# A mixed feed-forward whose ScalarE and VectorE read a step's banks first and split its weights second

## The chip, the cores and the metric

One core of a Trainium2 chip runs the whole program. The metric is the time of one execution in microseconds (us) of device time; the table below gives the median of several executions, and one further execution was profiled. TensorE (PE) does the matmuls, VectorE (DVE) and ScalarE (ACT) the elementwise work, GpSimd (POOL) some sums, and SyncE (SP) issues the loads from memory (HBM) into on-chip buffers.

## The reference, cut to what matters

Two model blocks run on 512 tokens of 1024 channels, in 32-bit floats. The part that the change touches is the feed-forward of the first block, with 4096 hidden channels:

```python
h = rmsnorm(x, norm_mlp_w[l]) * (1.0 + sc2) + sh2
ff = jnp.square(jax.nn.relu(h @ mlp_w1[l])) @ mlp_w2[l]
x = x + g2 * ff
```

Mixers stand before it and the whole second block behind it. Those stages stay as they are.

## The kernel before

**Precision by splitting.** Each 32-bit operand is split in two: ScalarE writes the rounded high part (`w_hi`, line 568 in the feed-forward), VectorE subtracts it from the original to get the low part (`w_lo`, line 577). PE then does three matmuls for each product (lines 484 to 486: high times high, low times high, high times low). So no weight can be used before ScalarE and then VectorE have passed over it.

**Items.** PE works through a list, ITEMS. Six "whole" items compute hidden tiles 0 to 5 (128 channels each; 24 matmuls of 512 columns). The other 26 hidden tiles are made in 13 pairs, 3 to 15, by a scheme that takes seven smaller products ("part" items 1 to 7, of 12 matmuls of 256 columns) for what would else be eight. Between the parts stand "down" items, which multiply finished hidden tiles with the second weight matrix (12 matmuls of 512 columns). A pair runs in this order: part 1, part 2, down, part 5, down, part 6, down, part 7, down, part 3, part 4. After pair 15 twelve down items remain.

**Buffers.** `raw` holds four tiles of 512 KB as they come from memory. SP issues their loads strictly in order, and each waits until the old contents of its place are split (and, for the first matrix, summed by GpSimd into `wsums`, which parts 3, 5, 6 and 7 use). Among the first loads in this stage SP's queue also holds eight loads of another matrix (`ada_a`, `ada_b`), each of which waits for a `gate_tile` on VectorE (line 2652, `acc<-ada,c_act,acc`). `w_hi` and `w_lo` have eight slots; a whole item takes two, the others one. `made_at` gives, at each item, the splits to be done in that step: those of the item seven slots ahead. The split waits only for the item that last used the slot, which is the one just before the item of the step. So it can run while PE is still on the item of the step.

**Bank reads.** PE sums into PSUM banks (`banks`). At a whole item ScalarE waits for PE to end it, then applies relu (L1915), squares (L1876) and makes the high part `hid_hi` (L1882). VectorE makes `hid_lo` of the tile before and then does a `gate_tile`. At parts 1, 5 and 6 ScalarE copies a bank to `snaps` (L1894); at parts 2, 7 and 3 VectorE adds a bank and a snap into `zt` (L2665, "block"). At part 3 and part 4 ScalarE does relu, square and `hid_hi` of a hidden tile. At a down item VectorE adds the bank onto `xT` (L2668). PE waits in turn: part 6 for the block of part 2, part 4 for the block of part 7, and part 1 of pair 3 for the relu of whole item 5 (its banks are 3 to 5). Between the first down item and part 5 of pair 3, PE sums the result of all eight `gate_tile`s (L790).

**Order.** Every engine's instructions are in program order, and a wait blocks all that stands behind it on its engine. In each step both ScalarE and VectorE first do the splits of the step and then its bank reads.

Of the kernel before, what the change touches and what calls it, by code (L numbers as in the profile page):

```python
# [211 lines left out]
def build(nc, a, out):  # L212
    with ExitStack() as ctx:
# [225 lines left out]
        def raw_wait(eng, d):  # L439
            eng.wait_ge(raw_in[d % RING], 16 * (d // RING + 1))  # L440

        def hi_unit(act, u, i=0):

            d = raw_index(u)
            act.wait_ge(raw_in[d % RING], 16 * (d // RING + 1) + 16 * i)
            if u >= RING:
                act.wait_ge(w_used, u - RING + 1 + RING * i)
            if U_V <= u < U_V + RING:
                act.wait_ge(f_used, SLOTS_END - SLOTS + 2 * (u - U_V + 1))
            src, dst = raw[:, d % RING, :], w_hi[:, u % RING, :]  # L450
            if u == 2:
                for s, t in index_parts(src, dst):
                    ins = act.activation(t, s, ACT.Copy)
                ins.then_inc(split_hi, 1)
            else:
                act.activation(dst, src, ACT.Copy).then_inc(split_hi, 1)  # L456
# [66 lines left out]
        def is_sum(item):  # L523
            return item[0] == "part" and FORM[item[2]][0] == "S"

        def sum_at(name):
            return wsums[:, S_ORDER.index(name), :]

        def sum_count(p, name):
            return N_TSUM + 4 * (p - FIRST_PAIR) + S_ORDER.index(name) + 1  # L530
# [21 lines left out]
        def slot_hi(act, item):  # L552

            if item[0] == "value":
                hi_unit(act, U_V + item[1])
                return
            n = SLOT[item]
            if n < SLOTS:
                act.wait_ge(w_used, U_FF - RING + n // 2 + 1)
            else:  # L560
                act.wait_ge(f_used, n - SLOTS + (2 if item[0] == "whole" else 1))
            if is_sum(item):
                act.wait_ge(ff_summed, sum_count(item[1], FORM[item[2]]))
                src = sum_at(FORM[item[2]])
            else:
                raw_wait(act, ff_raw(raw_of(item)))
                src = raw_part(item)
            act.activation(in_slot(w_hi, item), src, ACT.Copy).then_inc(f_hi, size_of(item))  # L568

        def slot_lo(dve, item):  # L570

            if item[0] == "value":
                lo_unit(dve, U_V + item[1])
                return
            dve.wait_ge(f_hi, SLOT[item] + size_of(item))
            src = sum_at(FORM[item[2]]) if is_sum(item) else raw_part(item)
            dve.tensor_tensor(in_slot(w_lo, item), src, in_slot(w_hi, item).bitcast(F32), ALU.subtract).then_inc(f_lo, size_of(item))  # L577
# [934 lines left out]
        def _(act):  # L1512
# [383 lines left out]
            def last_rows(j):  # L1896

                act.wait_ge(x_new, X_FF + j + 1)
                if j >= 2:
                    act.wait_ge(sq_added, Q_FF + j - 1)  # L1900
                act.activation(sqb[:, j % 2, :], xT[:, j, :], ACT.Square).then_inc(sq_made, 1)
                act.wait_ge(sq2_added, max(j + 1, 2))
                act.activation(relu[:, j % 2, :], xT[:, j, :], ACT.Square,
                               scale=par[:, PCOL["final_norm_w"] + j:PCOL["final_norm_w"] + j + 1]).then_inc(sq1_made, 1)
                act.activation(h_hi[:, j, :], xT[:, j, :], ACT.Copy, scale=scale4[:, j:j + 1]).then_inc(h_hi_made, 1)

            for item, now in made_at():
                for what in now:
                    slot_hi(act, what)
                kind, g = item[0], item[1]  # L1910
                if kind == "whole":
                    used(act, item)
                    if g >= 4:
                        act.wait_ge(h_ready, H_HID + g - 3)
                    act.activation(zt[:, g % 4, :], banks[:, g, :], ACT.Relu).then_inc(evac, 1)  # L1915
                    squared(g)
                elif kind == "part":
                    i = item[2]
                    if (g, i) == (FIRST_PAIR, 1):
                        form_highs()  # L1920
                    if i in (1, 5, 6):
                        snap(g, i, {1: 0, 5: 1, 6: 2}[i])
                    if i == 3:
                        z = zt[:, 2 * g % 4, :]
                        act.wait_ge(ff_added, added(g, 3))
                        act.activation(z, z, ACT.Relu).then_inc(evac, 1)
                        squared(2 * g)
                    if i == 4:
                        z = zt[:, 2 * g % 4 + 1, :]
                        used(act, item)  # L1930
                        act.wait_ge(h_ready, H_HID + 2 * g - 2)
                        act.activation(z[:, HALF:], z[:, HALF:], ACT.Relu)
                        act.activation(z[:, 0:HALF], part_bank(g, 4), ACT.Relu).then_inc(evac, 1)
                        squared(2 * g + 1)
                elif g == 7:
                    last_rows(item[2])

            def v_roots():

# [197 lines left out]
        def _(dve):  # L2137
# [533 lines left out]
            def last_rows(j):  # L2671

                used(dve, ("down", 7, j))
                if j == 0:
                    dve.wait_ge(ff_x, N_DOWN)
                onto_x(j, LAST_BANK[j]).then_inc(x_new, 1)
                dve.wait_ge(sq_made, Q_FF + j + 1)
                dve.wait_ge(sq_added, Q_FF + j)
                dve.tensor_tensor(ssq[:, :], ssq[:, :], sqb[:, j % 2, :], ALU.add).then_inc(sq_added, 1)
                dve.wait_ge(sq1_made, j + 1)  # L2680
                dve.wait_ge(sq2_added, 2 + j)
                dve.tensor_tensor(relu2[:, 0, :], relu2[:, 0, :], relu[:, j % 2, :], ALU.add).then_inc(sq2_added, 1)
                dve.wait_ge(h_hi_made, H_SGU + j + 1)
                dve.scalar_tensor_tensor(h_lo[:, j, :], xT[:, j, :], scale4[:, j:j + 1], h_hi[:, j, :].bitcast(F32),
                                         ALU.mult, ALU.subtract).then_inc(h_ready, 1)

            for item, now in made_at():
                for what in now:
                    slot_lo(dve, what)
                kind, g = item[0], item[1]  # L2690
                if kind == "whole":
                    if g:
                        hidden_low(g - 1)
                    gate_tile(g)
                elif kind == "part":
                    i = item[2]
                    if i == 1:
                        if g == FIRST_PAIR:
                            hidden_low(WHOLE - 1)
                            gate_tile(6)  # L2700
                            gate_tile(7)
                            form_lows((0, 1))
                        else:
                            hidden_low(2 * g - 2)
                    if i == 2:
                        block(g, 2, zt[:, 2 * g % 4, 0:HALF], 0, 1)
                        if g == FIRST_PAIR:
                            form_lows((2, 3))
                        else:
                            hidden_low(2 * g - 1)  # L2710
                    if i == 7:
                        block(g, 7, zt[:, 2 * g % 4 + 1, HALF:], 1, 2)
                    if i == 3:
                        block(g, 3, zt[:, 2 * g % 4, HALF:], 2, 3)
                elif g < 6:
                    m = KT * g + item[2]
                    if m == 0:
                        mod_part(6, 5, 1)
                        dve.wait_ge(mod_ready, 7)
                    used(dve, item)  # L2720
                    if m >= KT:
                        dve.wait_ge(ff_x, m - KT + 1)
                    onto_x(item[2], 6 + m % 2).then_inc(ff_x, 1)
                elif item == ("down", 6, 4):
                    hidden_low(HIDDEN - 2)
                    hidden_low(HIDDEN - 1)
                    dve.wait_ge(h_ready, H_HID + HIDDEN)
                    dve.memset(relu2[:, 0, :], 0.0).then_inc(sq2_added, 2)
                elif g == 7:
                    last_rows(item[2])  # L2730

# [447 lines left out]
```

## Time and profile before

| | us |
|---|---|
| median of 3 executions | 1298.34 (1297.82 to 1301.42) |
| the profiled execution, device time | 1300.62 |
| its span in the trace | 1299.0 |
| the mixed feed-forward in it | about 327 to 702 |

The profiled execution lies 2.28 us above the median, and 1.62 us of it lie outside its span. All times of day below are microseconds from the start of the span of this one execution.

How to read it: a row of a timeline has the start, the duration, the engine, the line, the operation and its names (output, then inputs). In brackets stand how long the engine was idle just before it and what ended that wait. In a table of stretches, each engine has its busy time, and PEclk is the clock granted to TensorE as a share of its full speed (1.00 is 2.4 GHz, 0.50 is 1.2 GHz).

### The profile page before, as it was taken

The page shows a single profiled execution, that of the slowest core. Times are in us where ns is not written, and L with a number is a line of the kernel's source. Part 1 is how long each engine was busy: PE and PEld are TensorE (multiplying, and loading weights), DVE is VectorE, ACT ScalarE, POOL GpSimd, SP SyncE. Part 2 cuts the span into 40 slices and gives each one's busy share as a digit, 9 for nine tenths or more (in the row PEclk, how much of TensorE's full clock was granted, in tenths as well). Part 3 has the DMA queues.
Part 4 walks back from the last instruction along what each step waited for, and adds up shares of the span by engine and source line. Part 5 has one row for each costly group of instructions (what it writes and reads, how often), then busy time and mean ns, then how long its engine had stood idle before and what let it go on. Part 6 is the DMA issues. An engine that isn't in the chain of part 4 may idle for free.

```text
span 1299.0 us, 19391 instructions
## 1 busy us (share of the span) xinstructions
PE 1240.9 (96%) x7048; PEld 1034.9 (80%) x7048; DVE 906.1 (70%) x1418; ACT 645.2 (50%) x1026; POOL 195.4 (15%) x220
## 2 busy tenths in 40 slices
PE   4999999999969999999899999999999999999998
PEld 3777778888758889888888888888888887777786
DVE  6889997856766655555657697766366667987832
ACT  3585345523544545454455565333233346978723
POOL 7022210000723131322300000110011001000000
PEclk9999999999979999999999999999999999999999
DMA  9678843325533232323233232334323232333311
GB/s 365 188 192 168 177 103 106 118 85 160 160 112 113 70 113 82 114 82 113 82 114 103 74 101 81 88 90 121 91 82 96 81 111 80 94 93 109 98 65 65
DMA packets 181614, 147.40 MB, mean 113 GB/s; under 512 B 6490, under 2 KB 162321, under 8 KB 181536
## 3 DMA queue, kind: packets, MB, share of 16 engines
q1 hardware_dynamic: 174064, 134.40, 33.7%
q0 software_dynamic: 6272, 10.91, 4.5%
q8 instruction: 49, 0.80, 0.2%
q10 hardware_dynamic: 1200, 1.05, 0.2%
q14 instruction: 29, 0.24, 0.1%
HBM read 135.59 MB, written 2.10 MB: 106 GB/s over the span
## 4 chain that ended last, share of the span: by engine, by line
PE 54%; DVE 23%; ACT 9%; issue 7%; DMA 6%; POOL 1%; ACTq 0%; DVEq 0%; SPq 0%; POOLq 0%
PE banks L484 16%; PE banks L486 16%; PE banks L485 16%; DMA raw<-in_mlp_w 4%; DVE w_lo L577 4%; DVE w_lo L468 2%; ACT w_hi L456 2%; ACT w_hi L568 1%; DVE xT L2668 1%; DVE score L2301 1%; DVE m L2298 1%; DVE xc L2902 1%; ACT zt L1876 1%; DVE score L2284 1%; DVE zt L2665 1%
## 5 line engine op out<-in xcount | busy, mean ns | idle before, releaser
L484 PE MATMUL banks<-h_hi,w_hi 128*128 128x512 f32 (+1 forms) x740 | 283.9, 384 | 10.0 <-ACT zt L1915 8.7
L486 PE MATMUL banks<-h_hi,w_lo 128*128 128x512 f32 (+1 forms) x740 | 274.5, 371 | 0.0
L485 PE MATMUL banks<-h_lo,w_hi 128*128 128x512 f32 (+1 forms) x740 | 274.2, 371 | 0.0
L468 DVE TENSOR_TENSOR w_lo<-raw,w_hi 128x1024 fp32r<-128x1024 f32 x136 | 165.5, 1222 | 88.9 <-ACT w_hi L456 86.5
L456 ACT ACTIVATE w_hi<-raw 128x1024 fp32r<-128x1024 f32 x136 | 142.2, 1051 | 100.0 <-PE banks L486 78.2
L484 PEld LDWEIGHTS banks<-h_hi,w_hi 128*128 128x128 f32 x740 | 142.0, 192 | 42.8 <-issue 17.1
L577 DVE TENSOR_TENSOR w_lo<-raw,w_hi 128x512 fp32r<-128x512 f32 (+1 forms) x109 | 93.3, 866 | 113.5 <-ACT w_hi L568 113.3
L485 PEld LDWEIGHTS banks<-h_lo,w_hi 128*128 128x128 f32 x740 | 142.2, 192 | 26.0 <-issue 3.8
L486 PEld LDWEIGHTS banks<-h_hi,w_lo 128*128 128x128 f32 x740 | 141.8, 192 | 23.5
L568 ACT ACTIVATE w_hi<-raw 128x512 fp32r<-128x512 f32 (+1 forms) x109 | 70.5, 648 | 98.1 <-DMA raw<-in_mlp_w 70.2
L484 PE MATMUL banks<-n_hi,w_hi 128*128 128x512 f32 x288 | 113.5, 394 | 0.9 <-DVE e L2864 0.9
L485 PE MATMUL banks<-n_lo,w_hi 128*128 128x512 f32 x288 | 112.1, 389 | 0.0
L486 PE MATMUL banks<-n_hi,w_lo 128*128 128x512 f32 x288 | 112.1, 389 | 0.0
L484 PE MATMUL banks<-hid_hi,w_hi 128*128 128x512 f32 x256 | 100.7, 393 | 3.0 <-DVE w_lo L577 1.6
L485 PE MATMUL banks<-hid_lo,w_hi 128*128 128x512 f32 x256 | 100.4, 392 | 0.0
L486 PE MATMUL banks<-hid_hi,w_lo 128*128 128x512 f32 x256 | 99.6, 389 | 0.0
L3136 POOL TENSOR_TENSOR e<-e 128x512 f32<-128x512 f32 x16 | 20.6, 1289 | 364.1 <-DVE e L2854 364.1
L484 PE MATMUL banks<-t_hi,w_hi 128*128 128x256 f32 x208 | 60.2, 289 | 11.1 <-DVE zt L2665 11.1
L3128 POOL TENSOR_TENSOR wsums<-raw 128x512 f32<-128x512 f32 x26 | 38.5, 1479 | 205.3 <-DMA raw<-in_mlp_w 205.3
L484 PEld LDWEIGHTS banks<-n_hi,w_hi 128*128 128x128 f32 x288 | 54.1, 188 | 11.8 <-issue 1.1
L484 PE MATMUL banks<-w_hi,h_hi 128*128 128x512 f32 x160 | 63.2, 395 | 0.0
L486 PEld LDWEIGHTS banks<-n_hi,w_lo 128*128 128x128 f32 x288 | 54.1, 188 | 11.3
(446 smaller groups left out, 2467.6 us busy)
## 6 DMA issues: line engine op xcount, KB each, us to landing
raw<-in_mlp_w SPq DMA_DIRECT2D x64, 512.0 KB, 4.9
raw<-in_a_w_in SPq DMA_DIRECT2D x48, 512.0 KB, 3.8
raw<-in_w_in SPq DMA_DIRECT2D x28, 512.0 KB, 4.4
raw<-in_ada_w SPq DMA_DIRECT2D x26, 512.0 KB, 4.3
raw<-in_b_w_in SPq DMA_DIRECT2D x24, 512.0 KB, 3.6
raw<-in_a_w_out SPq DMA_DIRECT2D x16, 512.0 KB, 3.5
raw<-in_b_w_out SPq DMA_DIRECT2D x12, 512.0 KB, 3.6
raw<-in_w_out SPq DMA_DIRECT2D x8, 512.0 KB, 4.2
```

Of the source, the lines that this page charges most:

```text
L456: act.activation(dst, src, ACT.Copy).then_inc(split_hi, 1)
L468: dve.tensor_tensor(dst, src, hi, ALU.subtract).then_inc(split_lo, 1)
L484: pe.matmul(dst, l_hi, r_hi, start=first, stop=False, skip_group_check=onto)
L485: pe.matmul(dst, l_hi, r_lo, start=False, stop=False, skip_group_check=onto)
L486: return pe.matmul(dst, l_lo, r_hi, start=False, stop=last, skip_group_check=onto)
L568: act.activation(in_slot(w_hi, item), src, ACT.Copy).then_inc(f_hi, size_of(item))
L577: dve.tensor_tensor(in_slot(w_lo, item), src, in_slot(w_hi, item).bitcast(F32), ALU.subtract).then_inc(f_lo, size_of(item))
L1876: act.activation(z, z, ACT.Square).then_inc(relu_sq, 1)
L2284: ins = dve.scalar_tensor_tensor(score[b][:, :], relus[:, i, 0:n], w, score[b][:, :], ALU.mult, ALU.add)
L2298: found[b] = chain.step(dve.max(m8[:, b - 1, :], score[b][:, :]))
L3128: pool.tensor_tensor(sum_at(name), left, right, op).then_inc(ff_summed, 1)
L3136: pool.tensor_tensor(e0[:, cc, :], e0[:, cc, :], e1[:, cc, :], ALU.mult).then_inc(ugp_made, 1)
```

## The change

In the two loops that walk over `made_at()`, on ScalarE and on VectorE, the splits of a step are moved behind the step's reads. Nothing is added or removed.

```diff
             for item, now in made_at():
-                for what in now:
-                    slot_hi(act, what)
                 kind, g = item[0], item[1]
...
                 elif g == 7:
                     last_rows(item[2])
+                for what in now:
+                    slot_hi(act, what)
...
             for item, now in made_at():
-                for what in now:
-                    slot_lo(dve, what)
                 kind, g = item[0], item[1]
...
                 elif g == 7:
                     last_rows(item[2])
+                for what in now:
+                    slot_lo(dve, what)
```

ScalarE at whole items 0 and 1, before. The rows of L568 are the splits of whole items 3 and 4.

```order
L568 ACTIVATE w_hi<-raw 128x1024
L1915 ACTIVATE zt<-banks 128x512
L1876 ACTIVATE zt<-zt 128x512
L1882 ACTIVATE hid_hi<-zt 128x512
L568 ACTIVATE w_hi<-raw 128x1024
L1915 ACTIVATE zt<-banks 128x512
```

The same place in the change (relu of a whole item is line 1913 there):

```order
L1913 ACTIVATE zt<-banks 128x512
L1876 ACTIVATE zt<-zt 128x512
L1882 ACTIVATE hid_hi<-zt 128x512
L568 ACTIVATE w_hi<-raw 128x1024
L1913 ACTIVATE zt<-banks 128x512
```

The first split of the stage, that of whole item 3, now stands behind the three operations on whole item 0.

VectorE at the same items, before. L2652 is `gate_tile`.

```order
L577 TENSOR_TENSOR w_lo<-raw,w_hi 128x1024
L2652 SCALAR_TENSOR_TENSOR acc<-ada_a,c_act,acc 128x1024
L577 TENSOR_TENSOR w_lo<-raw,w_hi 128x1024
L2659 TENSOR_TENSOR hid_lo<-zt,hid_hi 128x512
L2652 SCALAR_TENSOR_TENSOR acc<-ada_b,c_act,acc 128x1024
```

And in the change:

```order
L2652 SCALAR_TENSOR_TENSOR acc<-ada_a,c_act,acc 128x1024
L577 TENSOR_TENSOR w_lo<-raw,w_hi 128x1024
L2659 TENSOR_TENSOR hid_lo<-zt,hid_hi 128x512
L2652 SCALAR_TENSOR_TENSOR acc<-ada_b,c_act,acc 128x1024
L577 TENSOR_TENSOR w_lo<-raw,w_hi 128x1024
```

Each `gate_tile` has one split fewer ahead of it.

VectorE in the second half of pair 4, from the third down item to part 3, before (the later pairs up to 14 read alike). The splits are, in order, those for the next pair's part 2 and first down item (x2), part 5, second down item and part 6.

```order
L577 TENSOR_TENSOR w_lo<-raw,w_hi 128x512 x2
L2668 SCALAR_TENSOR_TENSOR xT<-banks,mod,xT 128x512
L577 TENSOR_TENSOR w_lo<-wsums,w_hi 128x512
L2665 TENSOR_TENSOR zt<-banks,snaps 128x256
L577 TENSOR_TENSOR w_lo<-raw,w_hi 128x512
L2668 SCALAR_TENSOR_TENSOR xT<-banks,mod,xT 128x512
L577 TENSOR_TENSOR w_lo<-wsums,w_hi 128x512
L2665 TENSOR_TENSOR zt<-banks,snaps 128x256
```

And in the change, from the same addition onto `xT` on:

```order
L2668 SCALAR_TENSOR_TENSOR xT<-banks,mod,xT 128x512
L577 TENSOR_TENSOR w_lo<-raw,w_hi 128x512
L2665 TENSOR_TENSOR zt<-banks,snaps 128x256
L577 TENSOR_TENSOR w_lo<-wsums,w_hi 128x512
L2668 SCALAR_TENSOR_TENSOR xT<-banks,mod,xT 128x512
L577 TENSOR_TENSOR w_lo<-raw,w_hi 128x512
L2665 TENSOR_TENSOR zt<-banks,snaps 128x256
L577 TENSOR_TENSOR w_lo<-wsums,w_hi 128x512
```

The addition onto `xT` now stands ahead of the split of the next pair's first down item, the first block (of part 7) ahead of that of its part 5, and the second block (of part 3) ahead of that of its part 6.

## Rows read from the trace of the kernel before

**Rows 1.** Waits, 340 to 690 us: waiter, releaser, us in total, times, longest.
```profile
ACT w_hi L568 <- DMA raw<-in_mlp_w: 68.0, 16, 7.0
PE banks L484 <- DVE zt L2665: 11.1, 9, 3.0
PE banks L484 <- ACT zt L1915: 8.7, 1, 8.7
PE banks L790 <- DVE acc L2652: 2.1, 1, 2.1
PE banks L484 <- DVE w_lo L577: 1.6, 1, 1.6
```

**Rows 2.** Table of stretches: length, busy us of each engine, clock, DMA share, GB/s.
```profile
369.00:374.00 5.00, 5.00 (x25) 5.00 (x25) 2.45 (x4) 1.03 (x3) 0.00 (x0) 0.50 0.90 263
...
381.00:386.00 5.00, 5.00 (x23) 4.56 (x23) 4.96 (x9) 0.90 (x2) 0.00 (x0) 0.67 0.00 0
...
466.00:470.00 4.00, 4.00 (x23) 4.00 (x22) 1.40 (x4) 2.71 (x6) 0.00 (x0) 0.57 0.05 16
487.00:509.00 22.00, 21.99 (x140) 19.86 (x140) 13.12 (x21) 10.91 (x22) 5.57 (x5) 1.00 0.31 96
```

**Rows 3.** Timeline of PE at three of its waits.
```profile
368.74 0.55 PE L484 MATMUL banks<-h_hi,w_hi 128*128 128x256 f32 x1 [8.68 <-ACT zt L1915]
...
380.87 0.56 PE L484 MATMUL banks<-t_hi,w_hi 128*128 128x256 f32 x1
...
440.80 0.36 PE L484 MATMUL banks<-t_hi,w_hi 128*128 128x256 f32 x1 [1.01 <-DVE zt L2665]
```

**Rows 4.** Timeline of ACT around the whole items.
```profile
335.73 1.05 ACT L568 ACTIVATE w_hi<-raw 128x1024 fp32r<-128x1024 f32 x1
342.41 0.60 ACT L1915 ACTIVATE zt<-banks 128x512 f32<-128x512 f32 x1 [5.63 <-PE banks L486]
...
364.11 0.63 ACT L568 ACTIVATE w_hi<-raw 128x512 fp32r<-128x512 f32 x1 [6.52 <-DMA raw<-in_mlp_w]
```

**Rows 5.** Timeline of DVE around the whole items.
```profile
338.85 1.67 DVE L577 TENSOR_TENSOR w_lo<-raw,w_hi 128x1024 fp32r<-128x1024 f32 x1
340.44 1.71 DVE L2652 SCALAR_TENSOR_TENSOR acc<-ada_a,c_act,acc 128x1024 f32<-128x1024 f32 x1
345.39 1.43 DVE L577 TENSOR_TENSOR w_lo<-raw,w_hi 128x1024 fp32r<-128x1024 f32 x1 [3.24 <-ACT w_hi L568]
...
367.18 1.27 DVE L2652 SCALAR_TENSOR_TENSOR acc<-ada_a,c_act,acc 128x1024 f32<-128x1024 f32 x1
```

**Rows 6.** Timeline of SP's queue: two loads of raw tiles, then three of pair 6.
```profile
358.92 0.43 SPq L753 DMA_DIRECT2D raw<-in_mlp_w  x1
...
368.85 0.43 SPq L753 DMA_DIRECT2D raw<-in_mlp_w  x1
...
431.41 1.54 SPq L753 DMA_DIRECT2D raw<-in_mlp_w  x3
```

**Rows 7.** Timeline of DVE in the second half of pair 5.
```profile
437.36 1.25 DVE L577 TENSOR_TENSOR w_lo<-raw,w_hi 128x512 fp32r<-128x512 f32 x1 [4.12 <-ACT w_hi L568]
438.54 0.74 DVE L2668 SCALAR_TENSOR_TENSOR xT<-banks,mod,xT 128x512 f32<-128x512 f32 x1
439.20 1.12 DVE L577 TENSOR_TENSOR w_lo<-wsums,w_hi 128x512 fp32r<-128x512 f32 x1
440.24 0.41 DVE L2665 TENSOR_TENSOR zt<-banks,snaps 128x256 f32<-128x256 f32 x1
...
442.59 0.67 DVE L577 TENSOR_TENSOR w_lo<-wsums,w_hi 128x512 fp32r<-128x512 f32 x1
443.19 0.41 DVE L2665 TENSOR_TENSOR zt<-banks,snaps 128x256 f32<-128x256 f32 x1
```

**Rows 8.** Timeline of ACT in the same stretch.
```profile
436.70 0.63 ACT L568 ACTIVATE w_hi<-raw 128x512 fp32r<-128x512 f32 x1 [4.85 <-DMA raw<-in_mlp_w]
...
443.63 0.63 ACT L1926 ACTIVATE zt<-zt 128x512 f32<-128x512 f32 x1 [4.60 <-DVE zt L2665]
```

## The prediction

> **What bounds the kernel now.** I read first who waits for whom in the mixed feed-forward [rows 1]. PE is idle there for some 23 us in a few places, and all but one of these waits end with ScalarE or VectorE reading a bank or summing a gate: 8.7 us once for the relu of whole item 5, 11.1 us in nine waits for a block (`zt`), 2.1 us for the last `gate_tile`, 1.6 us which the view puts on a split. This last one stands where the first down item of pair 15 needs a bank that ScalarE has just read, so I take it for that. ScalarE in its turn waits 68 us for raw tiles. Second, the granted clock [rows 2]: after three of these waits it falls, to 0.50, 0.67 and 0.57 of full speed. The fourth stretch there shows a pair without any wait: 22.0 us with 140 matmuls. A pair has 84 matmuls of 256 columns and 48 of 512, so 180 units of 256 columns, and the stretch holds some more; a unit then takes about 0.117 us and a pair 21.1 us. Third, the timelines around two of the waits tell what is late.
>
> At the whole items it is a ring through SP's queue. A raw tile is loaded at 358.92 [rows 6], ScalarE waits 6.52 us for it and splits it at 364.11 [rows 4], then VectorE splits and comes to its `gate_tile` at 367.18 [rows 5], and only that gate releases SP for the next load at 368.85 [rows 6]. ScalarE's relus of whole items 4 and 5 stand behind those splits, and PE waits for the second relu until 368.74 [rows 3].
>
> In a pair it is a longer ring: load at 431.41 [rows 6], high part at 436.70 [rows 8], low part at 437.36, an addition onto `xT`, another split, the block of part 7 at 440.24 [rows 7], for which PE waits until 440.80 [rows 3], more of the kind up to the block of part 3 at 443.19 [rows 7], ScalarE's work on two hidden tiles from 443.63 on [rows 8], four more splits and the next load. PE gives this ring nothing that comes last: the reads at 438.54 to 443.19 show no wait of their own in brackets, so their items are over before.
>
> **The change, part by part.** No instruction is added or taken away. Each read changes places with the splits of its own step.
>
> *First split, late.* The high part of whole item 3 was made at 335.73, while ScalarE had nothing else to do until 342.41 [rows 4]. Now it stands behind three operations on whole item 0, which can't begin before 342.41. At 0.6 us each they end at 344.3, the high part (1.05 us) at 345.4, and the low part takes the place at which another split stands now, 345.39 with 1.43 us [rows 5], and ends at 346.8. PE ends whole item 0 at 342.4 and items 1 and 2 three matmuls later each, so at 343.8. It waits 3.2 us. **+3.2 us.** For the clock after it I take the row at 466, which follows the 3.0 us wait [rows 1, 2]: 4 us at 0.57, so **+1.7 us**. If the clock stays up, this is zero.
>
> The Trainium skill (TensorE: Matmul & The Clock Gate, section HAM oscillation — how this bites in real kernels) says that waits between bursts of matmuls throttle PE again, so that the next burst starts cold. By it the new wait is paid twice, 4.9 us, without it 3.2 us; it speaks against this change. The row at 466 agrees.
>
> *The ring at the whole items, opened.* The first gate comes at 338.85 in place of 340.44 [rows 5], and SP's next load 1.6 us earlier. From 345.39 VectorE has three rounds of split (1.4), `hid_lo` (0.7) and gate (1.5) (operations of these sizes: [rows 5, 7]), 10.8 us, so the gate of whole item 3 ends at 356.2 and the load behind it goes out at 356.5, 2.4 us before 358.92. The next gate has no split ahead of it that waits for this load: its load follows at about 360.4 in place of 368.85, 8.4 us earlier. ScalarE's relus stand ahead of the splits too. PE runs whole items 3 to 5 from 346.9 for 3 x 24 matmuls at 0.23 us and 1.7 us of slow clock, to 365.1. ScalarE reads the bank at once, and part 1 of pair 3 starts at 365.9 in place of 368.74. The wait shrinks from 8.7 to 0.9: **-7.8 us**. With so short a wait ahead of them, the two parts that ran at 0.50 for 5 us [rows 2] run at full clock: **-2.5 us**. The sum over all gates then needs the last gate, which I work out by the same steps at 372.0, 0.4 us after PE's down item; 2.1 us become 0.4: **-1.7 us**. The slow stretch at 381 lost 5 x 0.33 = 1.65 us [rows 2]; the sums over the gates, light work, remain ahead of it, so I take half: **-0.8 us**. In pair 3 I find two short waits that were hidden, for the first addition onto `xT` and for the first block of part 7: **+0.9 us**. Front in all: 3.2 + 1.7 - 7.8 - 2.5 - 1.7 - 0.8 + 0.9 = **-7.0 us**.
>
> *The ring in the pairs, shorter.* The addition onto `xT` now stands ahead of the low part that waits for the load, where VectorE is idle for 4.12 us [rows 7]. That takes 0.66 us (438.54 to 439.20) out of the ring. The split before the block of part 3 goes behind it: 0.60 us (442.59 to 443.19). The ring is 1.26 us shorter, the mean of the nine waits is 11.1 / 9 = 1.23 us, so PE becomes the bound at 21.1 us a pair. Behind the block of part 3 ScalarE has one more split (0.5 us) before its second hidden tile, and one fewer after it; VectorE's list up to the split that frees the raw tile has the same length. The block of part 7, on which PE waits, moves by more, from 440.24 to 438.54, so its own row is no limit. Of the one wait of 3.0 us, behind a late load, I leave 1.0: **-10.1 us**. The clock lost 4 x 0.43 = 1.7 us after it [rows 2]; with a shorter wait I take **-1.0 us**. No other wait of this kind shows a fallen clock.
>
> *The tail.* The 1.6 us of pair 15 hang on ScalarE's second relu, which has as much ahead of it as before; it gains only from the earlier block: **-0.5 us**. In the last rows both engines do the same work per step and the splits stand seven slots ahead, some 19 us; I cost this at zero, covered by PE's down items. Without that cover it would be one split a step, 0.6 us.
>
> Sum: -7.0 - 10.1 - 1.0 - 0.5 = -18.6 us. On the profiled execution: 1300.62 - 18.6 = 1282.0; on the median, which is 2.28 us lower, 1298.34 - 18.6 = **1279.7 us**.
>
> **The rivals.**
> *Front only* (0.11): in the pairs the ring is held by something that I don't see, such as the loads (68 us of ScalarE's waits [rows 1]), and PE goes on waiting 1.2 us a pair. That leaves -7.0: 1291.
> *Pairs only* (0.09): the front's gain is eaten by the new wait, because the high part of whole item 4 also comes late and PE stops a second time (another 3.2 + 1.7 us) or the gate wait stays. That leaves the pairs' -11.6 and -2: 1285.
> *Slower* (0.04): ScalarE now makes the high part for part 4 only after the snap of part 5, which waits for PE's end of part 5; before it could go ahead of it. This split frees the raw tile. From the end of part 5 to the start of part 4 PE has three down items and parts 6, 7 and 3, 108 units or 12.6 us. The chain beside them: snap and high 0.9, low 0.7, load to high 5.3 (431.41 to 436.70), high 0.7, low 1.2, block 0.4: 9.2 us. It has 3.4 us to spare, and decides once loads take 3.4 us longer than 5.3. Had it 2.5 us too much, twelve pairs would lose 1.3 us each more than now, against the front's -7.0: 1298.3 - 7.0 + 15.6 = 1307. For it speaks only the single 3.0 us wait; against it, that loads in the other pairs are alike.
> *No effect* (0.04): new waits take just what the old ones gave, in front and pairs: 1298.
>
> **How the numbers follow.** The forecast has 0.72. Its best end: all waits of rows 1 but the new one go, 23.5 us, and all slow clocks, 5.8 us, against 3.2 us, so 26 us: 1272. The range reaches up to the front-only case, 1291. A change of 0.3%, 3.9 us, is about what a measurement of this kernel can tell. Faster by more: 0.72 + 0.11 + 0.09 = 0.92; within: 0.04; slower: 0.04.
>
> **What would show it.** In the profile after: a PE wait of about 3 us near 344, ended by VectorE's split of whole item 3; no PE wait of over 1.5 us for whole item 5's relu, and full clock from there to 374 or so; loads behind the gates no longer 10 us apart; in pairs 4 to 14 the nine waits for `zt` gone or under 0.3 us and pairs 21.1 us apart. I am wrong if PE waits at another item of each pair, if the new wait is repeated at whole items 4 and 5, or if ScalarE's waits for raw tiles grow by what PE gains.

## The result and the profile after

| | before | the change |
|---|---|---|
| median of 6 executions, us | 1299.42 (1297.82 to 1302.32) | 1290.57 (1289.17 to 1294.41) |
| the profiled execution, us | 1300.62 | 1290.24 |
| its span, us | 1299.0 | 1288.6 |

The ratio of the times is 0.9934, with a 95% interval of 0.9914 to 0.9953. The change is faster by 8.9 us, where 18.6 were forecast. The two profiled executions lie 10.4 us apart, and the sums below are made against that.

Who waits for whom, 330 to 690 us, of the kernel after, rows of PE. The columns are as in [rows 1]: waiter, releaser, us in total, times, longest.

```profile
PE banks L484 <- DVE w_lo L577: 5.1, 2, 3.0
PE banks L790 <- DVE acc L2652: 3.9, 1, 3.9
PE banks L484 <- DVE zt L2665: 2.2, 7, 0.5
PE banks L484 <- DVE hid_lo L2659: 1.4, 1, 1.4
PE banks L484 <- ACT zt L1913: 0.8, 1, 0.8
```

Against [rows 1], the wait for the relu fell from 8.7 to 0.8 us, and the nine waits for a block (11.1 us) became seven of 2.2 us in all. But the wait for the last gate rose from 2.1 to 3.9 us, and the row of `w_lo` from 1.6 to 5.1 us, of which 3.0 are the late first split and 2.1 the wait at pair 15.

The three waits on the timeline of PE that answer to [rows 3], and the new one:

```profile
347.59 0.73 PE L484 MATMUL banks<-h_hi,w_hi 128*128 128x512 f32 x1 [2.98 <-DVE w_lo L577]
...
366.59 0.35 PE L484 MATMUL banks<-h_hi,w_hi 128*128 128x256 f32 x1 [0.78 <-ACT zt L1913]
...
376.32 3.58 PE L790 MATMUL banks<-ones,acc 128*128 128x1 f32 x16 [3.87 <-DVE acc L2652]
...
502.46 0.36 PE L484 MATMUL banks<-t_hi,w_hi 128*128 128x256 f32 x1 [0.45 <-DVE zt L2665]
```

Table of stretches of the kernel after; the columns are as in [rows 2].

```profile
348.00:352.00 4.00, 4.00 (x12) 3.12 (x12) 4.00 (x5) 3.61 (x5) 4.00 (x3) 0.61 0.28 65
...
368.00:372.00 4.00, 4.00 (x26) 3.59 (x25) 4.00 (x5) 4.00 (x6) 1.79 (x2) 1.00 0.06 10
...
376.00:380.00 4.00, 3.68 (x17) 3.68 (x18) 4.00 (x7) 0.00 (x0) 0.00 (x0) 0.50 0.01 1
380.00:384.00 4.00, 4.00 (x16) 3.71 (x17) 3.96 (x7) 1.30 (x3) 0.00 (x0) 0.50 0.00 0
384.00:388.00 4.00, 4.00 (x22) 3.45 (x22) 2.29 (x4) 0.12 (x1) 0.00 (x0) 0.85 0.38 106
487.00:509.00 22.00, 21.55 (x135) 19.37 (x134) 13.88 (x21) 10.77 (x23) 5.97 (x4) 1.00 0.31 97
```

The last row is the stretch that had no wait in [rows 2]. Now it has 0.45 us of one. The row at 368 is at full clock, where [rows 2] has 0.50 at 369. The rows from 376 on are new: after the gate wait PE runs at 0.50 for 8 us and at 0.85 for 4 more.

Offsets from the first matmul of the stage (327.16 before, 328.01 after) place the difference. Each is the start of a matmul on PE's timeline less the start of that first one:

| from the first matmul of the stage to | before | after | difference |
|---|---|---|---|
| part 1 of pair 3 | 41.58 | 38.58 | -3.00 |
| part 5 of pair 3, behind the gates' sum | 53.71 | 51.74 | -1.97 |
| part 4 of pair 3 | 69.30 | 68.29 | -1.0 |
| part 4 of pair 15 | 338.46 | 327.21 | -11.25 |
| first matmul of the next stage | 374.20 | 362.95 | -11.25 |

From pair 3 to pair 15 the starts of part 4 lie apart, in us:

```
before  22.06 22.28 24.29 22.59 21.20 22.06 22.44 22.07 22.59 22.26 22.31 23.01
after   21.04 21.04 21.04 21.33 21.71 21.45 21.61 21.58 21.53 21.48 21.69 23.42
```

So the pairs brought about what was forecast, and the front almost nothing: 1.0 of 7.0 us. The stage itself began 0.85 us later in this profile, ahead of everything that was changed; that is why the spans differ by 10.4 us and not by 11.25.

### The profile page after: what moved, and what is told of

The parts are those of the page before. It is cut to its first block, busy times and chain, and to the rows that moved or that the text cites. A ratio compares the mean times of both kernels' runs of the same rounds, so it can differ in the third digit from the quotient of the medians.

```text
span 1288.6 us, 19391 instructions
## 1 busy us (share of the span) xinstructions
PE 1243.5 (96%) x7048; PEld 1036.3 (80%) x7048; DVE 911.8 (71%) x1418; ACT 642.3 (50%) x1026; POOL 199.6 (15%) x220
## 4 chain that ended last, share of the span: by engine, by line
PE 49%; DVE 24%; ACT 10%; issue 7%; DMA 6%; POOL 3%; SPq 0%; ACTq 0%; DVEq 0%; POOLq 0%
PE banks L484 15%; PE banks L486 14%; PE banks L485 14%; DVE w_lo L577 5%; DMA raw<-in_mlp_w 4%; DVE w_lo L468 2%; ACT w_hi L456 2%; ACT w_hi L568 2%; ACT zt L1876 1%; DVE score L2301 1%; DVE xT L2668 1%; DVE m L2298 1%; DVE zt L2665 1%; DVE xc L2902 1%; POOL hx L3108 1%
## 5 line engine op out<-in xcount | busy, mean ns | idle before, releaser
L577 DVE TENSOR_TENSOR w_lo<-raw,w_hi 128x512 fp32r<-128x512 f32 (+1 forms) x109 | 90.0, 836 | 74.4 <-ACT w_hi L568 74.4
L568 ACT ACTIVATE w_hi<-raw 128x512 fp32r<-128x512 f32 (+1 forms) x109 | 68.7, 646 | 63.0 <-DMA raw<-in_mlp_w 60.5
L577 DVE TENSOR_TENSOR w_lo<-wsums,w_hi 128x512 fp32r<-128x512 f32 x52 | 45.4, 874 | 31.5 <-ACT w_hi L568 31.5
```

## The experiments

Twelve kernels ran. Where a ratio is given, it is to the kernel before on the same chip, with its 95% interval. The change itself was run again among them.

> The change once more, as the mark beside which the other three of this call stand. The profiles taken of before and after put the gain at 10.4 us: 10.65 us between part 4 of pair 3 and part 4 of pair 14 (246.15 us before, 235.5 us after), about 1.0 us at the front, -0.4 us in the tail. If that holds, the ratio is about 0.992 to 0.993. If the part of the gain in the medians (8.85 us) is the true one, 0.993.

The ratio was 0.9929 (0.9916 to 0.9943), median 1291.2 us. In its profiled execution the waits of PE were alike (3.0 us for the last gate, nine for blocks of 3.7 us in all), and part 4 of pair 15 started at +329.96, 2.75 us later than in the other profile of the same kernel. So a difference of 2 or 3 us between two profiles says nothing by itself.

**The stages apart.** Both engines read first only at the six whole items, or only from pair 3 on:

```diff
             for item, now in made_at():
-                for what in now:
-                    slot_lo(dve, what)
                 kind, g = item[0], item[1]
+                reads_first = kind == "whole"
+                if not reads_first:
+                    for what in now:
+                        slot_lo(dve, what)
...
+                if reads_first:
+                    for what in now:
+                        slot_lo(dve, what)
```

and the same on ScalarE; in the second kernel the flag is `kind != "whole"`.

> Reads first at the six whole items only, on both engines; from pair 3 on the order of before. Theory: the front trades its gains for new losses (3.0 us wait at whole item 3, 3.9 us for the last gate, 10 us of half clock) and nets 0 to 2 us, so -1 us against before, with the nine waits for the block of part 7 back at about 1 us each. Rival (the prediction's front): -7 us.

> Reads first from pair 3 on only; the whole items as before. Theory: all of the gain of the change is in the pairs, so -10 us against before; PE waits 8.7 us for the relu of whole item 5 as before, pairs 4 to 7 take 21.0 to 21.1 us and later ones up to 21.6 us. Rival: part of the pairs' gain comes from the head start of the loads at the whole items, then -6 us or less.

Whole items only: 0.9986 (0.9973 to 0.9999), 1298.54 us. Pairs only: 0.994 (0.9926 to 0.9954), 1292.89 us. The second alone is as good as the whole change, as far as these runs can tell: the intervals overlap. In the first, part 5 of pair 3 starts at +52.15 and part 4 at +69.03, 0.3 us ahead of the kernel before, and the pairs have their old length (21.97, 24.15, 22.58 and so on) after a first one of 21.04. The change at the whole items moves PE's waits about, and hardly gains by it.

In one thing the expectation for the pairs-only kernel missed: its first pairs don't run at PE's own 21.04 us but take 21.46, 22.85, 21.25 and 21.58. From part 4 of pair 3 to that of pair 14 it saves 6.5 us against the kernel before, where the two profiles of the change save 10.65 and 8.8. So a part of the change's gain in the pairs, some 2 to 4 us, came from reading first at the whole items as well: the first three loads that the splits of pair 3 release go out at +57.0 and +57.3 in the change and at +58.6 here. Single profiles are a weak ground for a difference of this size.

**The engines apart.** VectorE reads first in all steps, ScalarE splits first as before:

```diff
 on VectorE
+                reads_first = True
 on ScalarE
+                reads_first = False
```

> VectorE reads first everywhere, ScalarE splits first as before. Theory of the ring (loads, high part, low part, additions, relus, next load): ScalarE's order of before keeps the high parts early, so VectorE no longer finds a split of part 7's weights late behind the second relu; the ring is shorter than after's 21.55 us by some 0.6 us at least and PE bounds the pairs at 21.04 us. PE does not wait at whole item 3 and waits about 5 us, not 8.7, before pair 3. Total -14 us against before, -4 against the change. Rival: ScalarE's reads-first order is what gives the gain; then 0 to -5 us.

The ratio was 0.9834 (0.9818 to 0.9851), median 1277.67 us: not 14 us faster, but 23. PE's waits in the feed-forward, 330 to 690 us, of this kernel:

```profile
PE banks L484 <- ACT zt L1915: 8.4, 1, 8.4
PE banks L484 <- DVE zt L2665: 1.5, 1, 1.5
```

and its row of the pair stretch:

```profile
487.00:509.00 22.00, 22.00 (x143) 20.04 (x142) 14.50 (x22) 11.65 (x22) 5.99 (x4) 1.00 0.35 108
```

PE waits 8.4 us for the relu, as before the change, and once more 1.5 us in pair 3. Behind that it doesn't wait at all: every pair takes 21.04 us (one 21.1), and the waits at the end, for pair 15 (1.6) and for the last `hid_lo` (1.4), are gone too. Against the profile before, 2.9 us are saved up to part 4 of pair 3, 14.65 from there to pair 14, 2.0 in pair 15 and 1.6 behind it; 2.3 more lie ahead of the stage, where nothing was changed. Once VectorE reads first, ScalarE's half of the change, which this kernel leaves out, costs 13.5 us (1291.2 to 1277.67). A kernel with ScalarE's half alone wasn't tried.

**ScalarE reads first where its relu was late, only there.** VectorE as above; ScalarE reads first at whole items 3 to 5:

```diff
 on ScalarE
+                reads_first = kind == "whole" and g >= 3
```

> VectorE reads first everywhere; ScalarE reads first only at whole items 3, 4 and 5, so that its relu of whole item 5 is not behind a split that waits for a load, and whole item 3's split is early. PE's wait of 8.4 us for that relu goes. Theory: the last gate (73 us on the clock of 300, at 372.2 to 373.5 in the run with VectorE alone) bounds the front, PE just waits there instead, and the time is that of VectorE alone within 2 us (0.983 to 0.985), perhaps worse by a longer cold stretch. Rival: the relu was the bound, and 6 to 8 us more are gained (0.978).

The ratio was 0.9838 (0.9817 to 0.9859), median 1279.55 us: the same as with VectorE alone. PE's waits in its profile:

```profile
PE banks L484 <- ACT zt L1917: 5.8, 1, 5.8
PE banks L790 <- DVE acc L2657: 2.6, 1, 2.6
```

The relu wait is 2.6 us shorter, and 2.6 us of waiting for the last gate stand behind it. What the relu no longer holds up, the gate does.

**The ring in the pairs, shortened by another edit.** VectorE makes the low parts of the two hidden tiles of the pair before (`hid_lo`, 0.6 us each) behind the split that frees the raw tile, not ahead of it. This touches no read and no other split. It was put into the kernel before and into the change:

```diff
 VectorE, step of part 1
-                            hidden_low(2 * g - 2)
 step of part 2
-                            hidden_low(2 * g - 1)
 step of part 6
+                    if i == 6 and g > FIRST_PAIR:
+                        hidden_low(2 * g - 2)
+                        hidden_low(2 * g - 1)
```

> The kernel before, with one edit: in pairs 4 to 15 VectorE makes the two hid_lo of the pair before after the split that frees the raw tile, not before it. This takes 2 x 0.6 us out of the ring load, high part, low part, additions, relus, split, load, and touches no order of reads and splits. Theory of the ring: 22.3 - 1.2 = 21.1 us, so the waits for the block of part 7 shrink from a mean of 1.2 us to about 0.1, and the gain is 9 to 12 us, ratio 0.991 to 0.993, as much as the change's. Rival: what the change gained in the pairs came from PE getting its blocks sooner, not from a shorter ring; then PE waits as before and nothing is gained.

> The change, with the same edit (the two hid_lo behind the split that frees the raw tile). The ring of the change takes 21.5 us a pair from pair 8 on. Theory: 21.5 - 1.2 is under PE's 21.04 us, so all pairs take 21.04 us and the 2.2 us of waits for the block and much of the 2.1 us wait in pair 15 go: 4 to 6 us less than the change, ratio 0.988 to 0.990. Rival: the pairs from 8 on are slower for another reason (loads, GpSimd); then 0 to 1 us.

In the kernel before: 0.9911 (0.9893 to 0.993), 1288.66 us; the pairs come 21.04 to 21.7 us apart and the last 22.98. This one edit brings as much as the whole change. In the change: 0.9859 (0.9836 to 0.9883), 1281.45 us, by the ratios some 9 us under the change, where 4 to 6 were expected. PE's waits in its profile:

```profile
PE banks L790 <- DVE acc L2657: 3.3, 1, 3.3
PE banks L484 <- DVE w_lo L577: 2.9, 1, 2.9
PE banks L484 <- DVE hid_lo L2664: 1.4, 1, 1.4
PE banks L484 <- ACT zt L1917: 0.8, 1, 0.8
```

No wait for a block is left (the row of `zt` is ScalarE's relu), the wait of pair 15 is gone (2.9 is the first split), and all pairs are 21.04 us apart. So in the change the ring was still the longer of the two, by less than the 1.2 us taken out here.

**The gates earlier.** In the step of whole item 4 VectorE makes gates 4 and 5, in that of whole item 5 gates 6 and 7; the last two stood in the step of part 1 of pair 3:

```diff
-                    gate_tile(g)
+                    for t in {4: (4, 5), 5: (6, 7)}.get(g, (g,)):
+                        gate_tile(t)
...
-                            gate_tile(6)
-                            gate_tile(7)
```

> The change, and on VectorE gate tiles 5 and 7 each one step earlier (4 and 5 at whole item 4, 6 and 7 at whole item 5). In the profile of the change the last gate began at 374.98, after a wait for its load, which gate 5 had released at 370.9, and PE waited 3.87 us for it and then ran at half clock until 386.5. Theory: this chain ate the front's gain. With gate 5 done near 364 its load lands near 368 and the last gate ends near 371; PE waits 0 to 1 us, and with the clock kept up the gain over the change is 5 to 8 us, ratio to before 0.987 to 0.989. Rival: the gates are made no earlier because VectorE is held up by GpSimd at the same time and by raw tiles: 0 to 2 us over the change.

The ratio was 0.9918 (0.99 to 0.9936), median 1290.45 us: the same as the change. Yet the front is shorter. On its timeline PE goes from the down item to the gates' sum at once, waits 1.1 us behind it, and then meets longer waits in pairs 4 and 5:

```profile
372.45 1.95 PE L790 MATMUL banks<-ones,acc 128*128 128x1 f32 x16
375.49 0.55 PE L484 MATMUL banks<-t_hi,w_hi 128*128 128x256 f32 x1 [1.09 <-DVE t_lo L2649]
...
414.77 0.36 PE L484 MATMUL banks<-t_hi,w_hi 128*128 128x256 f32 x1 [1.73 <-DVE zt L2670]
...
437.13 0.35 PE L484 MATMUL banks<-t_hi,w_hi 128*128 128x256 f32 x1 [1.09 <-DVE zt L2670]
```

Part 5 of pair 3 starts at +48.22 (after: +51.74), part 4 at +64.50 (after: +68.29), 3.8 us earlier. Then pairs 4 to 6 take 23.0, 22.36 and 22.69 us where the change had 21.04 each, and the 3.8 us are gone. The expectation of 5 to 8 us was wrong. It priced PE's clock, and not the ring of loads, which doesn't start earlier because PE does.

If that is so, the earlier front must pay once the ring is the shorter one. The same edit was added to three kernels that had done away with the ring's waits: to the one with late `hid_lo` in the change, to the one with VectorE alone, and to the one with ScalarE's whole items 3 to 5. A last kernel has all the edits (VectorE reads first, ScalarE at whole items 3 to 5, late `hid_lo`, early gates).

> The change with both edits: hid_lo behind the split that frees the raw tile, gate tiles 5 and 7 earlier. Alone, the second gave 1 us over the change, though part 4 of pair 3 came 3.8 us earlier: pairs 4 to 6 then took 22.4 to 23.0 us. Theory: the ring gave it back because it bounds the pairs; with the ring under 21.04 us PE keeps the 3.8 us, so 3 to 4 us less than with the first edit alone (0.986): ratio 0.982 to 0.984. Rival: pairs 4 to 6 are slow again for lack of loads, and the ratio stays at 0.985 to 0.987.

> VectorE alone reads first, gates 5 and 7 earlier. PE still waits 8.4 us for the relu of whole item 5 and comes to the last gate only when it is done, so the earlier gates are worth nothing: 0.982 to 0.985, the same as VectorE alone (0.983) within 1.5 us. If it is 3 us faster, the relu itself hangs on the gates' loads.

> VectorE reads first everywhere, ScalarE reads first at whole items 3 to 5 only, and gate tiles 5 and 7 one step earlier. With both bounds of the front lifted (relu of whole item 5, last gate) and the ring of the pairs shorter than PE's 21.04 us, the front's gain should now come through: part 5 of pair 3 about 46 us after the stage's first matmul (50.5 with VectorE alone), so 3 to 5 us less than VectorE alone, ratio 0.979 to 0.981. Rival: the ring starts no earlier and gives the gain back, as when the gates alone were moved in the change (front 3.8 us faster, total 1 us): then 0.983 to 0.985.

> All edits together: VectorE reads first, ScalarE only at whole items 3 to 5, gates 5 and 7 earlier, hid_lo behind the split that frees the raw tile. The pairs are bound by PE at 21.04 us already without the last edit, so it should give nothing over the first kernel of this call, within 1.5 us. If it is faster by more, the ring still costs something in pairs 3 and 4.

| kernel | without the early gates | with them |
|---|---|---|
| the change | 0.9934, 0.9929 | 0.9918 (0.99 to 0.9936) |
| the change, late `hid_lo` | 0.9859 (0.9836 to 0.9883) | 0.9831 (0.9813 to 0.9849) |
| VectorE alone | 0.9834 (0.9818 to 0.9851) | 0.9825 (0.9806 to 0.9844) |
| VectorE, ScalarE at whole items 3 to 5 | 0.9838 (0.9817 to 0.9859) | 0.9822 (0.9802 to 0.9843) |
| the last one, with late `hid_lo` | | 0.9818 (0.9798 to 0.9838) |

In the second row the early gates bring 2.7 us by the medians (1281.45 to 1278.77), and its pairs stay at 21.04 us (the last 21.46). The intervals touch, but the profile shows the gain kept: part 4 of pair 3 starts at +63.82 in place of +67.81, part 4 of pair 15 at +316.72 in place of +320.29. In the third row there is nothing to gain, as expected: that kernel waits 9.1 us for the relu first, and the gates are made by then. The fourth fell short of its expectation of 0.979 to 0.981. There PE still waits 5.5 us for the relu, and the rows of GpSimd and ScalarE ahead of it show why:

```profile
362.13 0.72 POOL L3124 TENSOR_TENSOR t_sum<-hx,t_sum 128x256 f32<-128x256 f32 x1
362.81 1.26 POOL L3137 TENSOR_TENSOR wsums<-raw 128x512 f32<-128x512 f32 x1
...
364.16 0.63 ACT L568 ACTIVATE w_hi<-wsums 128x512 fp32r<-128x512 f32 x1 [4.21 <-POOL wsums L3137]
364.69 0.58 ACT L1917 ACTIVATE zt<-banks 128x512 f32<-128x512 f32 x1
```

The relu stands behind a split that belongs to the step of the item before, and this one waits 4.21 us for GpSimd's sum. That sum waits for nothing that the profile shows: GpSimd comes to it straight from its sums of the activations (`t_sum`), which it does without a pause from 331.67 on, and the later of the two raw tiles was asked for at 350.74. So in this kernel it is GpSimd's own list that holds back the relu; no run moves that work. The six kernels between 0.9818 and 0.9838 can't be told apart. The best median is 1276.21 us, that of the last one, against 1290.57 of the change.

## Why the forecast was right in sign and too large

Where the difference lies can be told from the offsets. 18.6 us were forecast, and the two profiles differ by 10.4. Of the missing 8.2 us, 6.0 are in the front, 0.45 in pairs 4 to 14, 0.9 in pair 15 and the tail, and 0.85 are the later start of the stage. The medians, 8.9 us apart, give 1.5 us less than the profiles, which lies within the scatter of single executions in the table above. The steps that failed are the time of the last gate, on which most of the front's terms hang, the length of VectorE's list in the ring, and the adding up of front and pairs.

**Which engine bounds the pairs: right.** Behind pair 3, PE was bound to a ring that it isn't part of, and 21.04 us a pair (forecast 21.1) is what it takes when the ring is shorter. From part 4 of pair 3 to part 4 of pair 14 the change saves 246.15 - 235.50 = 10.65 us; 10.1 + 1.0 were forecast.

**The ring's length: wrong, and hidden in the sum.** The step reads "VectorE's list up to the split that frees the raw tile has the same length". It has one split more. The timeline of VectorE behind the block of part 3, of the kernel before, in pair 5, with SP's next load:

```profile
446.21 0.69 DVE L577 TENSOR_TENSOR w_lo<-raw,w_hi 128x512 fp32r<-128x512 f32 x1 [2.61 <-ACT w_hi L568]
448.69 0.69 DVE L577 TENSOR_TENSOR w_lo<-wsums,w_hi 128x512 fp32r<-128x512 f32 x1 [1.79 <-ACT w_hi L568]
...
452.70 1.29 DVE L577 TENSOR_TENSOR w_lo<-raw,w_hi 128x512 fp32r<-128x512 f32 x2
...
453.41 1.89 SPq L753 DMA_DIRECT2D raw<-in_mlp_w  x2
```

And of the change, in a pair bound by the ring:

```profile
516.11 23.00 SPq L753 DMA_DIRECT2D raw<-in_mlp_w  x7
...
526.74 0.41 DVE L2665 TENSOR_TENSOR zt<-banks,snaps 128x256 f32<-128x256 f32 x1
529.76 0.69 DVE L577 TENSOR_TENSOR w_lo<-wsums,w_hi 128x512 fp32r<-128x512 f32 x1 [2.61 <-ACT w_hi L568]
532.24 0.69 DVE L577 TENSOR_TENSOR w_lo<-raw,w_hi 128x512 fp32r<-128x512 f32 x1 [1.79 <-ACT w_hi L568]
...
536.85 0.68 DVE L577 TENSOR_TENSOR w_lo<-raw,w_hi 128x512 fp32r<-128x512 f32 x1
...
537.56 1.54 SPq L753 DMA_DIRECT2D raw<-in_mlp_w  x3
```

The reader is to see that the two waits are the same, 2.61 and 1.79 us, but the weights behind them are each one place further back: the split that had followed the first wait (`raw`) now follows the second. VectorE's splits follow ScalarE's, and ScalarE now makes each behind its relus. The forecast also gave ScalarE "one more split" before its second hidden tile; its timeline has one there in both kernels.

The first half of the ring came out as forecast: from the load to the block of part 3 it takes 11.78 us before (431.41 to 443.19) and 10.63 after (516.11 to 526.74), 1.15 less, forecast 1.26. The second half didn't. From the block of part 3 (443.19 in [rows 7], 526.74 here) to the load it takes 10.22 us before and 10.82 after, with five splits before and six after up to the one that frees the tile: 0.60 us more, one split. The 1.26 us that were to leave the ring became 0.66 by this count, and 0.55 by the two rings shown (22.00 and 21.45 us from load to load). The distances of the pairs say about the same: their mean before, pairs 4 to 14 without the two odd ones of 24.29 and 21.20, is 22.30, and after, in the pairs that the ring bounds (7 to 14), 21.55 us, so 0.75 us less. PE's waits there are up to 0.45 us (the row at 502.46 above), where under 0.3 was forecast. That the total of the pairs came out near the forecast is in part luck: pairs 4 to 6 ran at 21.04 us with the ring ahead of PE, and the odd pair of 24.29 us went whole. In the other profile of the change the same pairs save 8.8 us.

Two kernels bear out that the ring is what was left. With 1.2 us of other work taken out of the change's ring, every pair takes 21.04 us. It does so too with ScalarE's order kept. VectorE's list is then as long as in the change, but its first split behind the block of part 3 waits for nothing, because ScalarE has made the high part before its relus:

```profile
517.79 0.42 DVE L2665 TENSOR_TENSOR zt<-banks,snaps 128x256 f32<-128x256 f32 x1
518.13 0.68 DVE L577 TENSOR_TENSOR w_lo<-wsums,w_hi 128x512 fp32r<-128x512 f32 x1
```

**The late first split: right.** PE waits 2.98 us (forecast 3.2) and the clock is 0.61 over the 4 us behind it, 1.6 us lost (forecast 1.7). The high part starts at 345.12 (forecast 344.3, and the stage began 0.85 us later) behind three operations on whole item 0. The rule of the Trainium skill on waits between bursts (TensorE: Matmul & The Clock Gate, section HAM oscillation — how this bites in real kernels) holds here. The trace agrees with it by the clock of 0.61 behind the wait of 2.98 us.

**The relu of whole item 5: right.** The wait is 0.78 us, the forecast 0.9.

**The last gate: wrong, the step that cost the front.** It was to come 0.4 us after PE's down item, at 372.0. It came 3.87 us after, while the down item itself ended when it should, allowing for the later start of the stage. The timeline of VectorE over the last three gates of the kernel after, and SP's load for the last:

```profile
364.53 0.70 DVE L577 TENSOR_TENSOR w_lo<-raw,w_hi 128x512 fp32r<-128x512 f32 x1 [3.08 <-ACT w_hi L568]
365.44 1.48 DVE L577 TENSOR_TENSOR w_lo<-wsums,w_hi 128x512 fp32r<-128x512 f32 x1 [0.21 <-ACT w_hi L568]
366.84 1.79 DVE L2659 TENSOR_TENSOR hid_lo<-zt,hid_hi 128x512 fp32r<-128x512 f32 x1
368.56 2.31 DVE L2652 SCALAR_TENSOR_TENSOR acc<-ada_b,c_act,acc 128x1024 f32<-128x1024 f32 x1
...
374.98 1.28 DVE L2652 SCALAR_TENSOR_TENSOR acc<-ada_b,c_act,acc 128x1024 f32<-128x1024 f32 x1 [1.10 <-DMA ada_b<-in_ada_w]
...
370.90 0.33 SPq L756 DMA_DIRECT2D ada_b<-in_ada_w  x1
```

The sum costed a split of this size at 0.7, `hid_lo` at 0.7 and a gate at 1.5; between 365.4 and 370.8 they took 1.48, 1.79 and 2.31. That is 2.7 us more, of the 3.5 by which the last gate was late. The sign named beforehand, loads behind the gates no longer 10 us apart, failed at this one: 361.85 and 371.35. The gate at 368.56 frees the place of the last gate's matrix, so its load goes out at 370.90, and VectorE waits for it until 374.98. Two terms hung on this: the last wait (-1.7 forecast, +1.7 measured), and the clock behind it (-0.8 forecast; the two rows at 0.50 and the one at 0.85 lose 2.0 + 2.0 + 0.6 = 4.6 us in the change, against 1.65 before [rows 2], so +3.0). With the measured sizes the front's sum is 7.9 us saved at the relu and, as the half clock at 369 [rows 2] did go, 2.5 of clock, less 3.0 + 1.6 for the late first split, less 1.7 + 3.0 at the gate: 1.1 us remain, and 1.0 was measured. The kernel with early gates shows that the gates were the cause: part 5 starts 3.5 us earlier in it. What made the three operations slow is read off the timeline alone (GpSimd's sums beside them, last section); no run moves those sums.

**That front and pairs add up: wrong.** No term of the sum names this; it underlies all of them. PE waits for the longer of itself and the ring, so what PE gains ahead of the pairs counts only as far as the ring starts earlier too, or has slack. With the ring longer, the 3.8 us of the early gates were given back in three pairs. With it shorter, 3.6 of 4.0 us stayed. So had the last gate come as forecast, nearly 4 us would still have been missing in the change. How much a front that is faster by all of 7.0 us would keep isn't settled by these runs.

**The tail: wrong by 0.9 us.** The wait in pair 15 grew from 1.65 to 2.11 us, where -0.5 was forecast. The rows are, first before, then after, PE's wait and, from VectorE's timeline, the last split ahead of the block of part 3:

```profile
644.40 0.67 DVE L577 TENSOR_TENSOR w_lo<-wsums,w_hi 128x512 fp32r<-128x512 f32 x1
648.81 0.47 PE L484 MATMUL banks<-hid_hi,w_hi 128*128 128x512 f32 x1 [1.65 <-DVE w_lo L577]
...
633.58 1.12 DVE L577 TENSOR_TENSOR w_lo<-raw,w_hi 128x512 fp32r<-128x512 f32 x1
638.44 0.47 PE L484 MATMUL banks<-hid_hi,w_hi 128*128 128x512 f32 x1 [2.11 <-DVE w_lo L577]
```

From the block of part 3 to PE's matmul it takes 3.81 us in both, so ScalarE's second relu has as much ahead of it as before, and that the forecast had right. But PE's part 4 starts by the block of part 7, so the wait depends on the distance between the two blocks, and this grew from 2.95 us (642.05 to 645.00) to 3.39 (631.24 to 634.63), nearly all in the split shown. The earlier block of part 3 gained nothing, because that of part 7 came earlier too. The wait is gone where PE bounds the pairs, with VectorE alone and with late `hid_lo` in the change; with late `hid_lo` in the kernel before it is still 1.66 us.

**The rivals.** The slower one, a late high part for part 4, didn't show: no wait stands at part 4 of any pair but through the block. "Front only" names the measured time, 1291 for 1290.6, and that is chance: nearly all of the gain is in the pairs and 1.0 us in the front, the reverse of what it says, and ScalarE's waits for raw tiles (340 to 690 us) fell from 68.0 to 58.6 us. "Pairs only" had the mechanism nearest to what was measured, "or the gate wait stays", but named 1285.

## What to carry to other kernels

Where two engines pass the same tiles on in a fixed order, ask of each separately whether reading first pays. Here it did on the second engine of the pass, VectorE, whose idle time before a split lay ahead of reads that others needed. On the first, ScalarE, it cost, since what the first delays arrives later at the second: VectorE's half of the edit was worth 23 us, both halves together 9 us.

If the bound is a ring of loads, splits and reads without the matmuls in it, walk that ring once more in the new order and count every instruction from one load to the next. Time that the matmul engine saves ahead of such a ring doesn't count until the ring is the shorter one.

## What the hardware showed that was not expected

VectorE's operations on two SBUF operands took up to 2.6 times as long while GpSimd summed tiles (`wsums`, four operations from 363.38 on to 369.8): the split 1.48 us against 0.68 at 371.40, `hid_lo` 1.79 against 0.68 at 372.00, the gate 2.31 against 1.27 at 372.60. Not every one was slower: the split at 364.53 took 0.70 us beside such a sum. The rows of GpSimd in the kernel after:

```profile
363.38 1.30 POOL L3128 TENSOR_TENSOR wsums<-raw 128x512 f32<-128x512 f32 x1
364.76 1.61 POOL L3128 TENSOR_TENSOR wsums<-wsums,raw 128x512 f32<-128x512 f32 x1
366.33 1.75 POOL L3128 TENSOR_TENSOR wsums<-raw 128x512 f32<-128x512 f32 x1
368.05 1.74 POOL L3128 TENSOR_TENSOR wsums<-raw,wsums 128x512 f32<-128x512 f32 x1
```

The operations that take one operand from a PSUM bank kept their time beside such sums, in the pair shown above: the block 0.41 us at 523.35 and the addition onto `xT` 0.74 at 525.04, between splits of 1.31, 1.43 and 1.11 us. The Trainium skill (SBUF — State Buffer, section SBUF: two separate sides) says that a VectorE instruction with two SBUF inputs and a GpSimd instruction that reads SBUF exclude each other on a shared port. The trace agrees in so far as only such instructions are slowed here. It shows longer durations on both sides (GpSimd's 1.75 against 1.30), not which of the two blocked, and no run takes the one away from the other.

The clock around the sum over the gates, sixteen matmuls of one column, fell for longer when PE had waited longer there. Of five kernels, the time lost is each row's 4 us by the part of full clock that was not granted, summed over the rows shown:

| kernel | waited ahead of the sum, us, then behind it | granted clock in rows of 4 us | lost, us |
|---|---|---|---|
| VectorE, ScalarE at whole items 3 to 5, early gates | 0, then 0.5 | 1.00, 1.00 | 0 |
| the change, early gates | 0, then 1.1 | 0.88, 0.69 | 1.7 |
| before | 2.1 | 0.86, 0.72 | 1.7 |
| VectorE, ScalarE at whole items 3 to 5 | 2.6 | 0.69, 0.50, 0.95 | 3.4 |
| the change | 3.9 | 0.50, 0.50, 0.85 | 4.6 |

So here a wait of over 1 us cost 0.8 to 1.6 times as much again in clock, one of 0.5 us nothing. The loss doesn't grow evenly with the wait: counted the same way, the change run again (3.0 us) and the change with late `hid_lo` (3.3 us) lost 3.4 us, as 2.6 us did, and reading first at the whole items only (3.6 us) lost 5.1. The late first split, 2.98 us of waiting with full matmuls behind it, lost 1.6 us.
